# One gather for an expert's u and v row, a ring of 8 double slots, and weights worked out two rows at a time

## The reference

```python
q = (xt @ wq).reshape(t, PEER_HEADS, 2, PEER_HALF)            # 8 heads, two halves of 128
sc = jnp.einsum('thpc,pkc->thpk', q, subkeys)                 # 128 keys per half
sv, si = lax.top_k(sc, PEER_TOPK)                             # 16 best of each half
cand = sv[:, :, 0, :, None] + sv[:, :, 1, None, :]            # 256 sums
cidx = si[:, :, 0, :, None] * PEER_NKEYS + si[:, :, 1, None, :]
cs, cpos = lax.top_k(cand.reshape(t, PEER_HEADS, -1), PEER_TOPK)
idx = jnp.take_along_axis(cidx.reshape(t, PEER_HEADS, -1), cpos, axis=-1)
gate = jax.nn.softmax(cs, axis=-1)
act = jax.nn.gelu(jnp.einsum('td,tkd->tk', xbb, u_tab[ib]))   # 128 experts per token
y   = jnp.einsum('tk,tkd->td', gb * act, v_tab[ib])
```

## Time and profile before

| | |
|---|---|
| time, median of 3 runs | 1670.57 us |
| span of the profiled execution (first to last instruction) | 1667.8 us |
| TensorE matmul busy | 1367.3 us, 82% |
| VectorE busy | 1150.2 us, 69% |
| GpSimd busy | 1134.7 us, 68% |
| ScalarE busy | 441.8 us, 26% |
| mean granted TensorE clock | 0.923 |
| DMA | 607.17 MB, mean 364 GB/s; 180121 packets |

### The profile page before, as it was taken

How to read it: one execution, slowest core, us unless ns; L and a number is a source line. 1 busy time by engine, 2 the same in 40 slices (tenths; PEclk the granted TensorE clock), 3 DMA queues, 4 the chain that set the end, 5 groups by cost and what they waited for, 6 DMA issues and landing times.

```text
span 1667.8 us, 15134 instructions
## 1 busy us (share of the span) xinstructions
PE 1367.3 (82%) x3804; PEld 639.7 (38%) x3804; DVE 1150.2 (69%) x2826; ACT 441.8 (26%) x1065; POOL 1134.7 (68%) x1029
## 2 busy tenths in 40 slices
PE   7898988796976788979898868897988977776776
PEld 3443433343432344434343434444433422222222
DVE  2358775667466999996666699999566666666642
ACT  2313221122222343423211442342221321101111
POOL 0026777675777677767767757776777777777774
PEclk9989999997999898979999979997999989989899
DMA  9459999998999899989999989998999999999997
GB/s 360 146 193 350 406 409 402 408 405 348 392 406 409 331 347 348 346 318 389 406 406 404 406 334 334 361 351 323 402 406 405 398 371 393 380 358 373 372 395 271
DMA packets 180121, 607.17 MB, mean 364 GB/s; under 512 B 17488, under 2 KB 17616, under 8 KB 180048
## 3 DMA queue, kind: packets, MB, share of 16 engines
q0 software_dynamic: 147456, 536.94, 83.9%
q1 hardware_dynamic: 32592, 69.37, 11.1%
HBM read 605.19 MB, written 1.05 MB: 364 GB/s over the span
## 4 chain that ended last, share of the span: by engine, by line
PE 27%; DVE 25%; issue 14%; DMA 13%; POOL 12%; DVEq 5%; ACT 4%; POOLq 0%; ACTq 0%
PE ps L644 13%; PE ps L832 12%; POOL rings L386 12%; DVE rings L1205 11%; DMA rings<-in_v_tab_dram,idx 7%; DMA rings<-in_u_tab_dram,idx 5%; DVE mem L1086 2%; ACT dgs L594 2%; DVE mem L1089 1%; PE ps L636 1%; DVE mem L1077 1%; DVEq L1094 1%; DVEq L1079 1%; DVE mem L1078 1%; DVE mem L1080 1%
## 5 line engine op out<-in xcount | busy, mean ns | idle before, releaser
L832 PE MATMUL ps<-rings,dgs 128*128 128x512 f32 x2036 | 991.9, 637 | 246.2 <-DMA rings<-in_v_tab_dram,idx 135.2
L1205 DVE CUSTOM_DVE_ANT_0 rings<-rings,h 128x1024 f32<-128x1024 f32 x512 | 607.8, 1224 | 228.3 <-DMA rings<-in_u_tab_dram,idx 222.6
L386 POOL DMA_INDIRECT rings<-in_u_tab_dram,idx x512 | 575.0, 1123 | 255.8 <-issue 145.8
L386 POOL DMA_INDIRECT rings<-in_v_tab_dram,idx x512 | 558.4, 1091 | 224.7 <-issue 143.7
L832 PEld LDWEIGHTS ps<-rings,dgs 128*128 128x128 f32 x2036 | 397.0, 203 | 774.5 <-issue 624.0
L644 PE MATMUL ps<-wst,hT 128*128 128x512 f32 x384 | 174.7, 610 | 1.7 <-ACT hT L481 0.8
L594 ACT ACTIVATE dgs<-cst,wgt 128x128 f32<-128x128 f32 x512 | 153.0, 387 | 11.8 <-DVE wgt L1215 11.8
L579 ACT ACTIVATE gexp<-cs,ncs 128x16 f32<-128x16 f32 x32 | 9.8, 307 | 413.9 <-DVE pos_i L1176 413.9
L644 PEld LDWEIGHTS ps<-wst,hT 128*128 128x128 f32 x384 | 75.2, 197 | 97.6 <-issue 96.4
L584 ACT ACTIVATE gel<-dots 128x16 f32<-128x16 f32 x32 | 6.9, 216 | 298.7 <-DVE dots L1205 298.7
L791 PE MATMUL ps<-mem 128*128 128x32 f32 x512 | 68.4, 290 | 3.5 <-DVE mem L1090 3.5
(11 more groups left out here) (178 smaller groups left out, 935.8 us busy)
## 6 DMA issues: line engine op xcount, KB each, us to landing
wst<-in_wq_dram SPq DMA_DIRECT2D x15, 2048.0 KB, 18.8
wst<-in_w_out_dram SPq DMA_DIRECT2D x4, 2048.0 KB, 19.0
rings<-in_u_tab_dram,idx POOLq DMA_INDIRECT x512, 7.4
rings<-in_v_tab_dram,idx POOLq DMA_INDIRECT x512, 7.6
wst<-in_glu_w_dram SPq DMA_DIRECT2D x4, 2048.0 KB, 18.8
rings<-in_w_in_dram SPq DMA_DIRECT2D x3, 2048.0 KB, 16.6
vec<-in_vecs_dram SPq DMA_DIRECT2D x11, 512.0 KB, 6.9
rings<-in_w_in_dram SPq DMA_DIRECT2D x2, 1024.0 KB, 8.5
```

What stands on the lines that cost most here:

```text
L386: nc.gpsimd.indirect_dma_start(out=ring[:, s % RING, :], out_offset=None, in_=table, in_offset=bass.IndirectOffsetOnAxis(ap=idx[window][:, ...
L832: ins = PE.matmul(ps[:, 4 + 2 * t + b, :], diag[n % 2][:, s, :], ringv[:, s % RING, b * BANK:(b + 1) * BANK], start=(n % PH == 0 and s == ...
L1205: V.tensor_tensor_reduce(out=u, in0=u, in1=h[:, t, :], scale=1.0, scalar=0.0, op0=ALU.mult, op1=ALU.add, accum_out=dots[n % 2][:, s:s + 1] ...
```

## The change: what it does

- The two tables are laid side by side in memory (`uv_tab`, row = u then v, 8192 bytes). One indirect DMA per row fetches both. There are 512 in place of 1024, written out as a straight list.
- One ring of 8 slots of 8192 bytes per partition takes the place of two rings of 8 slots of 4096. The bytes of the ring are the same. A slot is free only when TensorE has multiplied its v half (`v_done`).
- ScalarE works out weights two rows at a time (`PACE` = 2): gelu of two dots, two products with the gate `share`, two diagonals. The gate is ready beforehand (`route_gate` on VectorE). There are 16 diagonals in place of 32.
- TensorE runs rows two behind the slot, not 16 behind.
- `route` is cut in five parts, run in slots 2, 4, 6, 8 and 10.
- Products can be issued in parts (`q_mm`, `z` with k0, k1). The sixth and seventh input products move partly into the prelude. Stages are shifted in the table; S5 pairs stand every 5 slots (slots 10 to 85 after the layer's start) in place of 4.4 (slots 20 to 86).
- `late_rows` is gone.

The diff, cut to what matters (of the table of stages and the straight renames only some lines stand):

```diff
-ROUTE_AT = 8
+PACE = 2
+DIAGS = 16
+ROUTE = {2: "route_keys", 4: "route_pairs", 6: "route_best", 8: "route_index", 10: "route_gate"}
+EXP_AT = 8
...
+           ("att_b", 0), ("norm_T", 1), ("sgu_b", 0), ("z", 5, 0, 3), ("mix", 0), ("mix_T", 0), ("z", 5, 3, 4),
+           ("w_out", 0, 0), ("w_out", 0, 1), ("z", 5, 4, 8), ("norm", 2), ("norm_T", 2), ("z_out", 5), ("z", 6, 0, 1),
+           ("q_mm", 0, 0, 0, 8), ("q_in", 0, 0), ("z", 6, 1, 2), ("q_turn", 0, 0), ("z", 6, 2, 3), ("q_score", 0, 0), ("z", 6, 3, 8)]
...
     def query(n, slot, phase, b):
-        for i, name in enumerate(("q_in", "q_turn", "q_score")):
-            at(n, slot + i, (name, phase, b))
+        at(n, slot, ("q_mm", phase, b, 0, 3))
+        at(n, slot + 1, ("q_mm", phase, b, 3, 6))
+        at(n, slot + 2, ("q_mm", phase, b, 6, 8), ("q_in", phase, b))
+        at(n, slot + 3, ("q_turn", phase, b))
+        at(n, slot + 4, ("q_score", phase, b))
...
-            slot = 20 + 22 * pair // 5
-            at(g + slot // TOPK, slot % TOPK, ("s5", t, pair))
-        at(g + 5, 9, ("s5_end", t))
...
+            at(g, 10 + 5 * pair, ("s5", t, pair))
+        at(g, 92, ("s5_end", t))
+        at(g, 94, ("gate_T", t))
+        at(g, 95, ("glu", t, 0))
+        at(g, 99, ("glu", t, 1))
+        at(g, 103, ("norm", 5 + 2 * t))
+        at(g, 106, ("norm_T", 5 + 2 * t))
+        query(g, 108, 2 + t, 0)
+        query(g, 114, 2 + t, 1)
+        query(g, 120, 2 + t, 2)
+        query(g, 128, 2 + t, 3)
...
@@ gpsimd
-                for s in range(0, TOPK, 2):
-                    pool.wait_ge(v_free, n * 16 + (s + 2))
-                    gather(ringv, v_tab, q, s, got_v)
-                    gather(ringv, v_tab, q, s + 1, got_v)
...
-                        pool.wait_ge(u_free, n * 16 + (s + 18))
-                        gather(ringu, u_tab, (q + 1) % 4, s, got_u)
-                        gather(ringu, u_tab, (q + 1) % 4, s + 1, got_u)
...
+            for g in range(GROUPS * TOPK):
+                n, s = g // TOPK, g % TOPK
+                if s == 0:
+                    pool.wait_ge(idx_ok, n + 1)
+                if g < RING and g % 2 == 0:
+                    pool.wait_ge(z_done, 6 + g // 2)
+                if g >= RING:
+                    pool.wait_ge(v_done, g - RING + 1)
                 nc.gpsimd.indirect_dma_start(
+                    out=ring[:, g % RING, :], out_offset=None, in_=uv_tab,
+                    in_offset=bass.IndirectOffsetOnAxis(ap=idx[n % 4][:, s:s + 1], axis=0)).then_inc(got[g % RING], 16)
@@ scalar
+            def weights(g):
+                n, i = g // TOPK, g // TOPK % 2
+                cols = [slice(s, s + 1) for s in range(g % TOPK, g % TOPK + PACE)]
+                every = slice(g % TOPK, g % TOPK + PACE)
...
+                act.wait_ge(dot_ok, g + PACE)
+                A.activation(gel[i][:, every], dots[i][:, every], ACT.Gelu_apprx_tanh)
+                act.drain()
+                for c in cols:
+                    A.activation(wgt[i][:, c], gel[i][:, c], ACT.Copy, scale=share[i][:, c])
+                act.drain()
+                for k, c in enumerate(cols):
+                    A.activation(diag[:, (g + k) % DIAGS, :], ident, ACT.Copy, scale=wgt[i][:, c]).then_inc(diag_ok, 1)
...
@@ tensor
+            def expert(g):
+                n, t = g // TOPK, g // TOPK // PH % T
...
+                pe.wait_ge(diag_ok, g + 1)
+                for b in range(2):
+                    ins = PE.matmul(ps[:, 4 + 2 * t + b, :], diag[:, g % DIAGS, :],
+                                    ring[:, g % RING, D + b * BANK:D + (b + 1) * BANK],
+                                    start=(g % (PH * TOPK) == 0), stop=(g % (PH * TOPK) == PH * TOPK - 1))
+                ins.then_inc(v_done, 1)
...
-            for n in range(1, GROUPS):
-                experts(n - 1, WORK[n])
-            experts(GROUPS - 1, {})
+            for g in range(GROUPS * TOPK):
+                run(WORK[g // TOPK].get(g % TOPK, []))
+                if g >= PACE and g % PACE == 0:
+                    for k in range(PACE):
+                        expert(g - PACE + k)
+            for k in range(PACE):
+                expert(GROUPS * TOPK - PACE + k)
@@ vector
+            def dot_product(g):
+                n, s, t = g // TOPK, g % TOPK, g // TOPK // PH % T
+                u = ring[:, g % RING, 0:D]
+                dve.wait_ge(got[g % RING], 16 * (g // RING + 1))
+                V.tensor_tensor_reduce(out=u, in0=u, in1=h[:, t, :], scale=1.0, scalar=0.0, op0=ALU.mult, op1=ALU.add,
+                                       accum_out=dots[n % 2][:, s:s + 1]).then_inc(dot_ok, 1)
...
+            for g in range(GROUPS * TOPK):
+                n, s = g // TOPK, g % TOPK
+                run(WORK[n].get(s, []))
+                if s in ROUTE and n + 1 < GROUPS:
+                    router[ROUTE[s]](n + 1)
+                dot_product(g)
```

More of the change, by code:

```diff
@@ L95, in between @@
     at(2, 6, ("sgu_b", 1))
-    at(3, 1, ("mix", 1))
-    at(3, 3, ("mix_T", 1))
-    at(3, 4, ("w_out", 1, 0))
-    at(3, 11, ("w_out", 1, 1))
-    at(4, 1, ("norm", 3))
-    at(4, 4, ("norm_T", 3))
-    query(4, 8, 0, 3)
-    query(4, 13, 1, 3)
+    at(2, 9, ("mix", 1))
+    at(2, 11, ("mix_T", 1))
+    at(2, 13, ("w_out", 1, 0))
+    at(3, 2, ("w_out", 1, 1))
+    at(3, 6, ("norm", 3))
+    at(3, 9, ("norm_T", 3))
+    query(3, 11, 0, 3)
+    query(4, 3, 1, 3)
     at(5, 2, ("s5_angle",))
@@ L198, in trunk @@
         sgb = sb("sgb", [P, 8])
-        ringu = rings[:, 0:RING * D].rearrange("p (b n) -> p b n", b=RING)
-        ringv = rings[:, RING * D:].rearrange("p (b n) -> p b n", b=RING)
+        ring = rings[:, :].rearrange("p (b n) -> p b n", b=RING)
         qs = part(8448, BANK)
@@ L215, in trunk @@
         idx = [sb(f"idx{i}", [P, TOPK], U32) for i in range(4)]
-        cs, gexp, dots, gel, wgt = (
-            [sb(f"{n}{i}", [P, TOPK]) for i in range(2)] for n in ("cs", "gexp", "dots", "gel", "wgt"))
+        cs, gexp, share, dots, gel, wgt = (
+            [sb(f"{n}{i}", [P, TOPK]) for i in range(2)] for n in ("cs", "gexp", "share", "dots", "gel", "wgt"))
         ncs, gsum, grec = ([sb(f"{n}{i}", [P, 1]) for i in range(2)] for n in ("ncs", "gsum", "grec"))
@@ L607, in _ @@
             gate_exp(0)
-            for n in range(GROUPS):
-                for s in range(TOPK):
-                    run(WORK[n].get(s, []))
-                    if s == ROUTE_AT and n + 1 < GROUPS:
-                        gate_exp(n + 1)
-                gelu(n)
-                diagonals(n)
+            for g in range(GROUPS * TOPK):
+                n, s = g // TOPK, g % TOPK
+                run(WORK[n].get(s, []))
+                if s == EXP_AT and n + 1 < GROUPS:
+                    gate_exp(n + 1)
+                if s % PACE == PACE - 1:
+                    weights(g + 1 - PACE)
             run(LAST)
@@ L637, in turn, with product @@
                 ins.then_inc(done, 1)
-            def product(bank, lhs, rhs, done, halves=False):
-                for k in range(KC):
+            def product(bank, lhs, rhs, done, k0=0, k1=KC, halves=False):
+                for k in range(k0, k1):
                     if halves and k == KC // 2:
@@ L846, in _ @@
             run(PRELUDE)
-            for slot in sorted(WORK[0]):
-                run(WORK[0][slot])
-            for n in range(1, GROUPS):
-                experts(n - 1, WORK[n])
-            experts(GROUPS - 1, {})
+            for g in range(GROUPS * TOPK):
[5 more added lines that the diff above has]
+                expert(GROUPS * TOPK - PACE + k)
         @block.vector
@@ L1180, in route @@
                 dve.drain()
-                hot = [c[:, :].rearrange("p (a b) -> p a b", a=TOPK) for c in (cand_a, cand_b)]
                 for p in range(2):
@@ L1225, in run @@
                         stage[name](*args)
-            V.memset(rden[:, 0:1], 0.0).then_inc(u_free, RING)
-            V.memset(rden[:, 1:2], 0.0).then_inc(v_free, RING)
             run(PRELUDE)
-            route(0)
-            for n in range(GROUPS):
-                dot_products(n)
-                weights(n)
+            for name in ROUTE.values():
+                router[name](0)
+            for g in range(GROUPS * TOPK):
+                n, s = g // TOPK, g % TOPK
+                run(WORK[n].get(s, []))
+                if s in ROUTE and n + 1 < GROUPS:
+                    router[ROUTE[s]](n + 1)
+                dot_product(g)
             run(LAST)
```

191 lines of the change are left out of this document (60 added, 131 removed).

## The result

The kernel after the change took 1709.45 us (median of 4 runs, 1707.23 to 1710.10), the kernel before beside it 1673.72 us (1670.47 to 1676.92). The ratio is 1.0206, 95% interval 1.0185 to 1.0228: slower. The record does not say which chip this was. The forecast was 1655 us, faster; its range for 8 in 10 ran from 1604 to 1706. Later runs of both on other chips gave another sign, since the kernel before was slower there (1741 to 1759 us) and the kernel after was not (1710). So there are two questions: why the kernel after isn't at 1655, and why the kernel before varies.

The account below looks back on a forecast made before the run. DMA bounds the ordinary stage, VectorE the S5 stage, GpSimd's issue the last PEER-only stretch. Terms -21, -16, -14, +34 and +1 sum to -16 us: span 1651.8, time 1654.6, rounded 1655 us; 8-in-10 range 1604 to 1706.

Parts of the forecast that it names:

- Issue by GpSimd: Last stretch, PEER rows only: halving the gathers to 512 brings issue per row below DMA time; -21 us, bounds -21 and 0.
- Packets: Gather queue where DMA is the bound: 73728 fewer packets at 5.2 ns each independent of size; -16 us, bounds -24 and 0.
- row is cut: Rival on the gathers: 8192 bytes go as two packets, time 1671, or 1692 if GpSimd's time doubles too; chance 0.10.
- S5 stage: S5 pairs, VectorE the bound: 5 slots per pair make a 14.2 us interval; -7 per layer tile, -14 us for two.
- Start and end: Prelude and tail: longer chain after the last landing +2.7, 1.7 given back, start 0; together +1 us.
- What the ring can cover: Slots held longer, so cover falls from 13.9 to 6.7 us and longer stalls cost time; +34 us, bounds 0 and about 98.
- Norms and the attention of tile 1: Stalls of 5 to 8 us at these stages, set against the smaller ring cover; 5 us in all.
- S5 setup: Setup before S5, 375 to 416 us, where DMA already lost 5.8 us: cover shrinks by 7.2 us; +7 us.
- GLU: Four GLU products: VectorE away 15 us instead of 9.7, behind two rows on TensorE; 4 us each, 16 in all.
- Route and gelu: Route in parts on VectorE hidden by DMA outside S5; ScalarE gets 150 us more work, off the path; 0 us.
- the queries use up the cover: Slower rival at VectorE's copy in `q_turn`, behind TensorE: each of 16 queries costs 4 us, +64, time 1719; chance 0.24.
- The ring covers all: Rival: weight blocks fill the DMA holes and the packet saving is whole (-24); -58 us, time 1612; chance 0.26.

## Why the prediction was wrong

The steps of the forecast, one by one:

- *Issue by GpSimd, -21:* right. A gather stayed at 1107 ns, and the last seven groups ran 30 us faster, which is this term and the share of the packets there. With two gathers a row, and all else as after, 26 of the 30 were lost again.
- *Packets, -16:* right in kind, and half the size. 73,728 packets, as foreseen if 8192 bytes stay whole, and 421 GB/s in place of 406 is 3.7%, 0.09 us, for every row that DMA bounds; the forecast had 24 us over 512 rows, 0.05 each. Its 5.2 ns per packet came from a mean size of 3641 bytes, but that queue holds 16 short packets beside the 128 rows of each gather. The gathers' queue before and after gives 152 ns for 3641 bytes and 292 ns (0.789 x 16 x 1705.5 / 73728) for 7282, so 12 ns without size. The Trainium skill, "DMA: Bandwidth & Descriptors", section on SWDGE vs HWDGE vs iDMA, prefers packets of at most 4096 bytes; no run here compares that for other transfers, and for these gathers the rate rose beyond that size, so the rival built on it (row is cut, 1671 or 1692) fell.
- *S5 stage, -14:* right. VectorE in order of time, the first and the last pair of tile 0, which answer to the earlier trace rows:

```profile
580.74 0.69 DVE L1050 TENSOR_TENSOR mem<-ps,mem 128x512 f32<-128x512 f32 x1 [2.63 <-ACT mem L512]
...
792.87 0.69 DVE L1050 TENSOR_TENSOR mem<-ps,mem 128x512 f32<-128x512 f32 x1
```

  15 intervals took 212.1 us; 213 was forecast.
- *Start and end, +1:* measured -9 + 18 - 20 = -11. The two ends of the 16-row lead were not both counted, an error of 12 on the good side. The end of the chain (start us, us, what), which answers to the earlier trace rows:

```profile
1678.12 13.28 DMA rings<-in_uv_tab_dram,idx
1694.25 3.71 PE ps L813 x8
...
1701.15 1.28 DVE h L850
```

- *What the ring can cover, +34:* this step failed. Take the terms above out of the 38 us: 38 + 30 + 11 + 15 = 94 us are left. They are the ring and the stalls, less what packets saved outside the last seven groups (11 us by the forecast, 21 by the measured rates). So the term was 105 to 115, three times its size. The cover itself, 6.7 us, was about right, as the route in one piece shows. The failed assumption is the length of the stalls: it set them as long as they had been, "some 5 each, under the cover: 0" for the queries. They became 9.4 us each, above the cover, for pairs of rows that only just became ready now stand in front of the hand-overs; one such hand-over was shown in order of time, and the spreading bears it out. "Norms and the attention of tile 1: 5 in all" failed the same way: groups 1 to 3, which hold them, the first queries and the w_out products (a wait of 10.8 us on average for each of the two, 4.8 before), lost 46 us. And with the steps spread, in a ring of the same 8 slots, 109 us came back, as much as the whole term, though a part of that may be the GLU and w_out products, which ran in one piece before the change too. So it was in the main the stalls, lengthened by the order of the steps, and not the depth of the ring; one slot less costs 35 and 38 us on top. The +7 for the S5 setup did not come: group 6, which holds it, took 51.3 us against 52.3.
- *GLU, 16:* VectorE's wait in the GLU, before 25.9 us for four, one of them in the earlier trace rows, is now

```profile
DVE mem L1111 <- PE ps L627: 42.6, 4, 12.3
```

  which is 4.2 us more each. The forecast had VectorE away 15 us in place of 9.7, so 5.3 more, and priced that at 4 each; the wait is about right, what time it cost isn't measured apart from the rest.
- *Route and gelu, 0:* ScalarE grew by 230 us and not by 150: 92 table loads where there were 60, at 1.28 us, and 512 products of 287 ns that I had put at 200. It is busy for 39% of the span and no bound; but it matters where its blocks stand.

Of the rivals, "the queries use up the cover" (1719) came nearest to 1709 and had one of the places right, VectorE's copy behind TensorE. It had the condition wrong: with u three rows ahead the loss in groups 0 to 3 was the same. And it put all 64 us on the queries, where attention, norms and w_out of tile 1 lost too; that its number came so near is in part luck. "The ring covers all" (1612) was refuted by slices 5 to 9. The forecast named as its own refutation "ScalarE's waits for other stages hold rows up"; what happened is the reverse, rows' waits on ScalarE hold the stages up, and those hold the rows of all engines.

Against the kernel before as it runs on chip C the change is a gain: after over before 0.9694 (0.961 to 0.9778). On chips B and D, where the kernel before is slow too, the kernel after didn't run. The forecast of 1655 is not saved by that, as the kernel after takes 1710 there too.

The fastest version is the change with its hand-overs spread, 1600.22 and 1602.03 us: 0.919 (0.9119 to 0.9261) and 0.9073 (0.8996 to 0.9151) of the kernel before on chips B and C, and 0.936 (1600.22 / 1709.45) of the kernel after. Its GB/s by slice:

```profile
GB/s 359 174 240 408 378 399 421 414 419 376 416 342 416 337 347 369 377 376 375 412 414 414 413 368 339 363 361 349 385 414 415 417 412 421 421 421 422 421 421 246
```

What is left is the prelude, the S5 stages with VectorE at 93% (209.30 of 225 us), and the last slice.

## What to carry to other kernels

When work is moved closer to the point where it becomes ready (rows two behind in place of sixteen), an in-order engine that shares its queue between that work and a chain of stages may wait for it in front of the chain: price each hand-over of the chain anew, not only the buffer that covers it. Then give every engine's step of a stage its own place in the order, late enough that its input is there, and cut long products so that rows fit between the parts; here that cost no instruction and was worth 109 us. And compare a kernel on more than one chip before a difference of a few per cent is called its own.

## What the runs showed of the hardware that was not expected

- Indirect gathers of 8192 bytes per partition go as one packet and reach up to 423 GB/s in a slice of the page, those of 4096 bytes at most 410 (the spread kernel with two gathers). GpSimd issues either in 1.1 us.
- Kernels with two gathers a row took 47 to 87 us longer on some chips, with waits of up to 14 us on VectorE that have no visible cause. The two kernels with one gather a row that ran on two chips took the same time on both within 2 us.
- With half of the row products left out, the granted clock fell from 0.93 to 0.81: TensorE waited for ScalarE's diagonals 174 times, 481 us in all, in place of 136 times and 278 us.
